# A two-block network on one core: weight units asked for one at a time in the layer end and the recurrence too

## The reference, cut to what matters

```python
proj = x @ w_in                                   # layer 1: 8208 columns
y = concat([conv_part, rms_norm(delta_rule(q, k, v, g, beta), g) * silu(z_b)])
s = y @ w_out
...
q_raw, f_raw, i_in, z = split(x @ w_in, 4)        # layer 2: 8192 columns
s = (rms_norm(hgrn2_recurrence(q, k, i_in, logf), g) * silu(z)) @ w_out
...
x = layer_norm(ALPHA * x + s, ln_g, ln_b)         # layer end, both layers
gate = sigmoid(x @ w_pl_gate)
x = x + (p @ w_pl) * gate
```

## Time and profile before

| what | value |
|---|---|
| median of 3 runs | 1275.89 us (1275.82 to 1279.35) |
| the profiled execution's own time | 1275.92 us |
| its span | 1274.1 us |
| TensorE busy | 1256.3 us (99%) |
| VectorE busy | 982.4 us (77%) |
| ScalarE busy | 768.6 us (60%) |
| moved by DMA | 247.51 MB, mean 194 GB/s |
| delta rule, its weights issued | 61 to 279 us |
| units 46 to 86 issued | 279.8 to 541.2 us |

### The profile page before, as it was taken

The page is one execution under the profiler, slowest core; times in us unless marked ns, Lnnn a source line. Parts: engine busy times, 40 slices in busy tenths (PEclk is TensorE's granted clock), DMA queues, the critical chain, the costliest instruction groups (busy, mean ns, idle before and its releaser), DMA issues.

```text
span 1274.1 us, 29857 instructions
## 1 busy us (share of the span) xinstructions
PE 1256.3 (99%) x12986; PEld 1147.8 (90%) x12986; DVE 982.4 (77%) x1539; ACT 768.6 (60%) x1075; POOL 28.3 (2%) x66
## 2 busy tenths in 40 slices
PE   9999999999999999999999999999999999999998
PEld 9999898999899999999987779888888888988887
DVE  5878768766788999998778988898787775986543
ACT  6867344474755666666564256876346885778431
POOL 0000000000000000000000000000000000000000
PEclk9999999999999999999999999999999999999999
DMA  8453444546466566564332254688864333665551
GB/s 316 176 185 133 146 178 178 202 164 223 166 254 236 207 216 230 218 216 150 133 133 101 101 199 166 246 338 319 309 243 164 138 128 110 251 248 211 186 187 64
DMA packets 34947, 247.51 MB, mean 194 GB/s; under 512 B 3904, under 2 KB 3904, under 8 KB 5504
## 3 DMA queue, kind: packets, MB, share of 16 engines
q1 hardware_dynamic: 29104, 204.96, 44.2%
q0 software_dynamic: 5712, 40.63, 8.6%
HBM read 244.53 MB, written 1.05 MB: 193 GB/s over the span
## 4 chain that ended last, share of the span: by engine, by line
PE 83%; DVE 9%; ACT 5%; issue 2%; POOL 0%; DVEq 0%; ACTq 0%; POOLq 0%
PE PS L511 17%; PE PS L512 9%; PE PS L427 9%; PE PS L428 8%; PE PS L429 8%; PE PS L528 5%; DVE WL L661 3%; ACT WH L628 2%; PE PS L443 2%; DVE BIG L306 2%; PE PS L1136 2%; PE PS L444 2%; PE PS L445 2%; PE PS L510 1%; PE PS L1061 1%
## 5 line engine op out<-in xcount | busy, mean ns | idle before, releaser
L661 DVE TENSOR_TENSOR WL<-RAW,WH 128x2048 fp32r<-128x2048 f32 x166 | 379.6, 2288 | 98.1 <-ACT WH L628 94.4
L628 ACT ACTIVATE WH<-RAW 128x2048 fp32r<-128x2048 f32 x166 | 316.8, 1909 | 139.6 <-PE PS L512 66.3
L427 PE MATMUL PS<-XW,WH 128*128 128x256 f32 x928 | 267.8, 289 | 0.2 <-DVE X L306 0.2
L428 PE MATMUL PS<-XW,WH 128*128 128x256 f32 x928 | 262.5, 283 | 1.3 <-issue 1.3
L429 PE MATMUL PS<-XW,WL 128*128 128x256 f32 x928 | 262.2, 283 | 0.3 <-issue 0.3
L427 PEld LDWEIGHTS PS<-XW,WH 128*128 128x128 f32 x928 | 177.5, 191 | 3.4 <-issue 1.9
L428 PEld LDWEIGHTS PS<-XW,WH 128*128 128x128 f32 x928 | 177.7, 191 | 1.7 <-issue 1.5
L429 PEld LDWEIGHTS PS<-XW,WL 128*128 128x128 f32 x928 | 177.5, 191 | 0.0
L511 PE MATMUL PS<-XW,WH 128*128 128x512 f32 x392 | 141.1, 399 | 0.2
L511 PE MATMUL PS<-YW,WH 128*128 128x512 f32 x368 | 129.9, 395 | 0.0
L306 DVE SCALAR_TENSOR_TENSOR BIG<-BIG,C 128x256 f32<-128x256 f32 (+2 forms) x232 | 102.9, 502 | 10.1 <-ACT BIG L1363 5.4
(11 more groups left out here) (449 smaller groups left out, 2586.0 us busy)
## 6 DMA issues: line engine op xcount, KB each, us to landing
RAW<-wst SPq DMA_DIRECT2D x191, 1024.0 KB, 4.8
BIG<-wad POOLq DMA_DIRECT2D x38, 1024.0 KB, 5.2
X<-xT SPq DMA_DIRECT2D x2, 512.0 KB, 4.8
RAW<-wst SPq DMA_DIRECT2D x2, 512.0 KB, 6.6
outT<-X SPq DMA_DIRECT2D x4, 256.0 KB, 4.2
K<-cst SPq DMA_DIRECT2D x1, 608.0 KB
CB<-crow SPq DMA_DIRECT2D x1, 512.0 KB
BIG<-pT POOLq DMA_DIRECT2D x2, 256.0 KB, 4.7
```

Of the source, the lines that this page charges most:

```text
L427: pe.matmul(o, h, hl[0][:, k0 + k, :], start=(k == 0), stop=False)
L428: pe.matmul(o, h, hl[1][:, k0 + k, :], start=False, stop=False)
L628: ac.activation(WH[p % NS][:, :], RAW[u % NR][:, :], ACT.Copy).then_inc(S.hi.tick(p), 1)
L661: ve.tensor_tensor(WL[p % NS][:, :], RAW[u % NR][:, :], WH[p % NS][:, :].bitcast(f32), ALU.subtract).then_inc(S.lo.tick(p), 1)
```

## The change

`alone` ends at the unit of ("oc", 0), which is 87, instead of the unit of ("ob", 0), which is 46. So units 46 to 86 too are each asked for only when the unit before has landed; they hold the last products of layer 1, layer end 0 and the projections of the whole recurrence.

```diff
         def sync_program(sp):
             taps = {direct["glu", 5]: 1, direct["glu", 7] + 3: 7}
-            alone = range(slots[where["a1", 0]][0], slots[where["ob", 0]][0])
+            alone = range(slots[where["a1", 0]][0], slots[where["oc", 0]][0])
```

## The result

The changed kernel takes 1279.91 us (median of 18 runs, 1277.79 to 1283.59), the kernel before beside it 1276.17 us (18 runs, 1274.80 to 1279.35). The ratio is 1.0029, 95% interval 1.0023 to 1.0036: slower by 3.7 us, and clear of noise. The prediction said 1276.2 us, with 1278.5 as the end of its range.

A forecast was written before the change was run, and what follows sets the result against it. TensorE was taken to bound the kernel from end to end, with 0.55 us idle in the stretch. Costs of 0.3 + 0 + 0 = 0.3 us on 1275.9 gave 1276.2 us, range 1274.9 to 1278.5 us.

The forecast's parts named there:

- What bounds, and what there is to win: Whole kernel: TensorE bounds it end to end; in the changed stretch lone transfers can win 0.55 us at most.
- Which issues move: Units 46 to 86: 14 are issued later, all before 400 us; from 400 us on nothing moves, cost 0, gain 0.
- some 14 more places where SyncE waits for RAW: Sign in the profile after, at the added line: some 14 more SyncE waits, longest 5 us, all before 400 us.
- Place A: Train at 282.6 us, before k = 4 of ("ob", 0): late copy of unit 48 stalls TensorE by 0.3 us.
- I take 5.4 us: Landing time of unit 48 beside pT and late, between the lone median 4.8 us and today's 6.4 us; stall 0.3 us.
- My own sign of being wrong: A TensorE stall over 2 us anywhere in the stretch of the change would show the prediction wrong.
- Places B and C: Layer end (units 54 to 56) and head pair 1 (60, 61): cost 0 each; at 6.3 us landings, 1.2 and 1.4 us.
- a late landing blocks ScalarE at A: Slower rival, train at 282.6 us: unit 48's copy holds up the zb copies; 4.1 us, so 1280.0 us; chance 0.06.

## Why the prediction was wrong

- **What bounds, and what there is to win: right.** TensorE from end to end, 0.55 us to win in the stretch. Nothing was won, and every kernel that kept unit 47's early issue, freed ScalarE or held POOL's transfers back came back to the time of before.
- **Which issues move: right.** From unit 68 on the issues keep their distances: 69 goes out at 422.91 instead of 416.57 and 71 at 436.73 instead of 430.39, both 6.34 us later. What I had named as a sign, some 14 more places where SyncE waits for RAW, could not show it: the view puts each wait at the added line down to a landing, 75 of them in all, met or not. The longest is 7.4 us, not 5.
- **Place A: here it failed, in two terms.** The step "Unit 46 lands at 284.65, 47 at 284.7 + 4.8, 48 at 289.5 + 4.8" and then "I take 5.4 us". 47 took 6.1 us and 48 took 7.5, so the copy started at 298.57 instead of the 294.3 to 294.9 that I had. I gave a lone transfer the median of 34, though their spread to 6.3 stood in the same row, and in a train of lone transfers each one's excess is handed to the next; why 47 in particular is slow stays open. And I let pT and late cost 48 0.6 us; issued 2.1 us ahead of it they cost 2.7, as it takes 7.5 us behind them and 4.8 with them out of the way. The way from the copy to TensorE was right to a tenth: 298.57 + 3.1 = 301.7, measured 301.78. The second term was missing: I priced a pause at its length. In the profiled run A cost 3.3 + 2.85 = 6.15 us, and 2.85 of them were clock. My own sign of being wrong, a stall of TensorE over 2 us, came true.
- **Places B and C: right.** Units 55 and 56 land in 4.7 and 4.8 us and 56 is copied at 351.84, 7.3 us later than before where TensorE is 6.6 us late, so 0.8 us of ScalarE's cover went; 61 is copied on its landing at 379.78 after ScalarE idled 0.07 us. No pause of TensorE follows either, and without 46 to 48 the rest of the change is at 0.9999, about 1 us of interval on either side.
- **The rivals.** The slower one, "a late landing blocks ScalarE at A", was the mechanism, to the line. That its price, 4.1 us, lies near the measured 3.7 us is luck in part: it was a pause alone, behind one landing of 9.3 us, and the measured cost is a shorter pause, 2.7 to 3.3 us in the two profiles that have it, with the clock behind it. I gave it 0.06 because I asked for one landing of 8.9 us; two of 6.1 and 7.5 in a row do the same. It was a matter of chances, not of a missing idea: two ordinary delays and the clock together reach what one rare delay would.

## What to carry to other kernels

Before a transfer is made to wait for another, look at what the in-order engine that consumes it has behind it, and count the slack against a train of landings at their upper end, with the other queues' transfers in front. A wait that is good in one stage (here around two pauses that end with "issue") is good for what it cures there; look for that pause in the stage to which it is extended. And a pause of a busy TensorE, even of one to two microseconds, may be followed by the lower clock: allow for more than its length, and look at the clock of every run. Whether matmuls of no use in the pause pay for themselves isn't shown here: the clocks were better with them, and the interval of the filling alone includes 1.

## What the runs showed of the hardware

- **The clock behind short pauses.** Pauses of 1.9, 2.45, 2.7, 3.3 and 5.5 us on an otherwise busy TensorE were each followed by a stretch at the lower level, 1.2 GHz, in some execution, and so were the pauses of 1.4 and 1.5 us in the delta rule. The same pause need not be: the one of 2.4 us in the attention layer was followed by it in the profile after and not in that of before. The kernel before takes some 2 us more at 0.997 than at 1.000 (medians of six runs each).
- **Instructions come by DMA too.** The profile before has 103 packets of instructions on queue q8, 1.69 MB, 16 KB each, beside the weights. With units queued behind each other such a packet starts 1.4 us later and TensorE stands 3.3 us, with lone ones 1.3 us. That the pause is a wait for this packet is read from its times, not tried. The Trainium skill, "Runtime: NRT & Kernel Launch", section "Instruction fetch mechanics", says that the fetch is hidden by the time that issuing takes. If the two pauses are such waits, it is not hidden in this kernel's delta rule, by 1.3 us at L428 with lone units and 3.3 us with queued ones.
- **A transfer behind POOL's.** Two transfers of 256 KB on POOL's queue, the first issued 2.1 us ahead, made a unit of 1 MB land in 7.5 us instead of 4.8; 1.7 to 1.8 us ahead, in 6.4 to 7.1 us.
